# First block's last mixer products, norm and feed-forward input, done by halves of the tokens

## The reference

```python
y = jnp.concatenate([y_a, y_b, y_c], axis=-1) @ w_out[l]
x = x + gt1 * y
h = rms_norm(x, norm_ffn[l]) * (1.0 + sc2) + sh2
x = x + gt2 * conv_glu_ffn(h, ffn_w_up[l], ffn_conv_w[l], ffn_conv_b[l], ffn_w_down[l])
```

## Time and profile before

| | us |
|---|---|
| median of 3 runs (lowest, highest) | 2663.39 (2656.81, 2664.59) |
| the profiled execution, its own time | 2664.73 |
| its span | 2662.9 |
| PE busy | 2486.4 (93%) |
| DVE busy | 1452.2 (55%) |
| ACT, POOL busy | 876.1, 871.6 (33% each) |

### The profile page before, as it was taken

The page is one execution under the profiler, slowest core; times in us unless marked ns, Lnnn a source line. Parts: engine busy times, 40 slices in busy tenths (PEclk is TensorE's granted clock), DMA queues, the critical chain, the costliest instruction groups (busy, mean ns, idle before and its releaser), DMA issues.

```text
span 2662.9 us, 36956 instructions
## 1 busy us (share of the span) xinstructions
PE 2486.4 (93%) x15164; PEld 1455.5 (55%) x15164; DVE 1452.2 (55%) x1697; ACT 876.1 (33%) x1082; POOL 871.6 (33%) x494
## 2 busy tenths in 40 slices
PE   5899999999889999999998889999888999999996
PEld 2555558886445555555554556675344555555552
DVE  5764666773486630566325687355486640466413
ACT  3255422221144520445213222321155531354303
POOL 0212110000236531555215767201226532455320
PEclk7999999999989999999998889989999999999998
DMA  7611020000301133111312612300111122211311
GB/s 322 236 41 44 17 107 3 3 3 16 118 9 64 48 105 125 64 48 59 118 69 104 103 48 70 136 1 24 56 72 48 64 87 104 87 64 48 118 33 63
DMA packets 53497, 196.29 MB, mean 74 GB/s; under 512 B 5585, under 2 KB 15313, under 8 KB 50385
## 3 DMA queue, kind: packets, MB, share of 16 engines
q1 hardware_dynamic: 45552, 176.38, 19.5%
q10 hardware_dynamic: 7776, 17.56, 1.9%
HBM read 164.55 MB, written 29.36 MB: 73 GB/s over the span
## 4 chain that ended last, share of the span: by engine, by line
PE 80%; DVE 10%; issue 2%; POOL 2%; DMA 2%; ACT 2%; SPq 0%; ACTq 0%; DVEq 0%; POOLq 0%
PE pt L1138 15%; PE pt L1144 15%; PE pt L1141 15%; PE pt L1680 11%; PE pt L573 7%; PE pt L411 3%; PE pt L714 2%; PE pt L2391 2%; PE pt L2397 2%; PE pt L2394 2%; DVE work L536 1%; PE pt L344 1%; DMA work<-in_w_mod 1%; PE pt L332 1%; PE pt L397 1%
## 5 line engine op out<-in xcount | busy, mean ns | idle before, releaser
L1088 POOL TENSOR_TENSOR slots<-work,weights_rounded 128x512 bf16<-128x512 f32 (+2 forms) x234 | 420.7, 1798 | 598.5 <-ACT weights_rounded L1247 309.0
L1141 PE MATMUL pt<-work,weights_rounded 128*128 128x512 bf16 x1248 | 334.8, 386 | 0.0
L1138 PE MATMUL pt<-rounded,weights_rounded 128*128 128x512 f32 x624 | 210.1, 453 | 15.8 <-POOL slots L1088 10.2
L1138 PE MATMUL pt<-rhs_rounded,weights_rounded 128*128 128x512 f32 x624 | 210.2, 453 | 12.0 <-POOL slots L1088 7.8
L573 PE MATMUL pt<-work 64*64 64x64 f32 (+5 forms) x4512 | 208.0, 240 | 6.5 <-DVE work L536 5.5
L1138 PE MATMUL pt<-hidden_rounded,weights_rounded 128*128 128x512 f32 x704 | 207.2, 427 | 0.4
L573 PEld LDWEIGHTS pt<-work 64*64 64x64 f32 (+3 forms) x4512 | 188.7, 138 | 26.0 <-DVE work L536 7.7
L1141 PEld LDWEIGHTS pt<-work,weights_rounded 128*128 128x128 bf16 x1248 | 100.1, 99 | 169.0 <-issue 98.1
L1144 PE MATMUL pt<-hidden_rounded,slots 128*128 128x512 bf16 x704 | 179.9, 387 | 0.0
L1141 PE MATMUL pt<-slots,weights_rounded 128*128 128x512 bf16 x704 | 174.4, 381 | 0.0
L1144 PE MATMUL pt<-rounded,slots 128*128 128x512 bf16 x624 | 171.2, 390 | 0.0
(11 more groups left out here) (368 smaller groups left out, 4112.2 us busy)
## 6 DMA issues: line engine op xcount, KB each, us to landing
work<-in_w_up SPq DMA_DIRECT2D x64, 512.0 KB, 4.0
work<-in_w_down SPq DMA_DIRECT2D x32, 704.0 KB, 4.0
work<-in_w_mod SPq DMA_DIRECT2D x10, 2048.0 KB, 8.7
slots<-in_w_in SPq DMA_DIRECT2D x31, 512.0 KB, 3.6
slots<-in_w_up SPq DMA_DIRECT2D x24, 512.0 KB, 4.8
x_scratch<-work ACTq DMA_DIRECT2D x16, 512.0 KB, 2.6
work<-x_scratch SPq DMA_DIRECT2D x16, 512.0 KB, 8.0
slots<-in_w_v SPq DMA_DIRECT2D x10, 512.0 KB, 4.3
```

The source lines that it names most:

```text
L1088: did(pool, pool.tensor_tensor(dst, raw, high.bitcast(F32), ALU.subtract), name)
L1138: pe.matmul(out, whi[:, k * P:k * P + P], rhs_hi(k), start=first and k == ks[0], stop=False, skip_group_check=True)
L1141: pe.matmul(out, top_half(whi)[:, k * P:k * P + P], rhs_lo(k), start=False, stop=False, skip_group_check=True)
```

## The change

The eight products f are now formed for the first 512 tokens first (`f_part(0)` to `f_part(7)`) and then for the last 512 (`f_part(8)` to `f_part(15)`), one PSUM bank each. The sums and the spreading of 1/rms exist once for each half: `sums(0)` stands behind part 9, `rows(0)` behind part 10, `sums(1)` and `rows(1)` inside `ffn_pe`, as `between`. DVE and ACT handle 512 tokens in each operation, and DVE's list mixes the second half's additions with the first half's norm. In `ffn_pe`, plain group 0 is formed for the first half with whole tiles (24 matmuls for the gate, 24 for the value), and only its second half goes slice by slice.

POOL no longer waits for f4: it splits the two weight tiles of group 0 as soon as they are loaded, with their rests in slot 32. The tile after these, (1, 0), now waits until six slices of the second half are split. So that nothing else lives in those slots, `XP` moves from slots 42, 43, 44, 45, 46 to 44, 45, 46, 3, 4; slots 3 and 4 are free only when the mixer's recurrent core is done, so their DMA is issued after that. Apart from this the places of some tiles in the second block are moved, and some semaphores are merged.

```diff
-        XP = (42, 43, 44, 45, 46, 30, 31, 47)
+        XP = (44, 45, 46, 3, 4, 30, 31, 47)
...
+                    sp.wait_ge(E("chunk_done"), 3 * NC)
+                    sp.dma_start(W[:, XP[3]:XP[3] + 2, :], a["xT"][:, 3:5, :]).then_inc(E("x_in1"), 16)
...
-            for m in range(8):
-                linear(pe, f"f{m}", lambda k, m=m: woc[:, m, k * P:(k + 1) * P], YC,
-                       (lambda: pe.wait_ge(E("woc_in"), 128)) if m == 0 else None, ("y_c", 0) if m == 0 else None)
-            pe.wait_ge(E("square_sums"), 7)
-            token_sums(pe, "ss2", w(SQ2[0]), const("ones")[:, 0:1], 1)
-            token_rows(pe, "rb2", ("rstd_sqrt", 2), one_row)
-            ffn_pe(pe, 0)
+
+            def f_part(i):
+                h, m = divmod(i, 8)
+                if i < 8 and i % 2 == 0:
+                    claim(pe, f"f{i // 2}")
+                elif 8 <= i < 12:
+                    half_wait(pe, "dve", ("f", i - 4))
+                elif i >= 12:
+                    pe.wait_ge(E("pt_emptied_dve"), ordinal[f"f{i - 12}"])
+                if i == 0:
+                    pe.wait_ge(E("woc_in"), 128)
+                for k in range(3):
+                    if i == 0:
+                        pe.wait_ge(E("y_c"), k + 1)
+                    ins = pe.matmul(f_bank(i), woc[:, m, k * P:(k + 1) * P], w(YC[k])[:, half_of(h)], start=(k == 0),
+                                    stop=(k == 2))
+                ins.then_inc(E("pt_filled" if h else "half_pe"), 1)
+
+            def sums(h):
+                if h:
+                    pe.wait_ge(E("square_sums"), 7)
+                else:
+                    half_wait(pe, "dve", ("acc", 7))
+                for st in range(4):
+                    at = 512 * h + st * P
+                    ins = pe.matmul(f_sums(h)[:, st:st + 1], w(SQ2[0])[:, at:at + P], const("ones")[:, 0:1], start=True,
+                                    stop=True, skip_group_check=True)
+                ins.then_inc(E("pt_filled" if h else "half_pe"), 1)
+
+            def rows(h):
+                if h:
+                    pe.wait_ge(E("rstd_sqrt"), 2)
+                else:
+                    half_wait(pe, "act", "sqrt")
+                for st in range(4):
+                    ins = pe.matmul(f_rows(h)[:, st * P:(st + 1) * P], one_row(4 * h + st), const("ident"), start=True,
+                                    stop=True, skip_group_check=True)
+                ins.then_inc(E("pt_filled" if h else "half_pe"), 1)
+
+            for i in range(16):
+                f_part(i)
+                if i == 9:
+                    sums(0)
+                if i == 10:
+                    rows(0)
+            ffn_pe(pe, 0, (lambda: sums(1), lambda: rows(1)))
...
             for m in range(8):
-                filled(dve, f"f{m}")
-                V_(dve.scalar_tensor_tensor(w(X + m), pt(f"f{m}")[:, :], small(MOD + 16 + m), w(XP[m]), ALU.mult, ALU.add),
-                   "pt_emptied_dve")
-                add_square(dve, SQ2, 8, m - 1)
-            add_square(dve, SQ2, 8, 7)
-            rstd_dve(dve, "ss2", 1.0 / D, EPS)
-            filled(dve, "rb2")
+                f_added(0, m)
+                if m > 1:
+                    f_square(0, m - 1)
+            f_square(0, 7)
+            for m in range(8):
+                f_added(1, m)
+                if m > 1:
+                    f_square(1, m - 1)
+                if m == 1:
+                    f_recip(0)
+                if 4 <= m < 7:
+                    f_low(0, 2 * m - 8)
+                    f_low(0, 2 * m - 7)
+                for k in {3: (0, 1), 4: (2, 3), 5: (4, 5), 6: (6,)}.get(m, ()):
+                    f_scaled(0, k)
+            f_square(1, 7)
+            f_scaled(0, 7)
+            f_low(0, 6)
+            f_low(0, 7)
+            f_recip(1)
...
             for k in range(9):
                 if k < 8:
-                    V_(dve.scalar_tensor_tensor(w(SQ2[k]), w(X + k), small(G2 + k), pt("rb2")[:, :], ALU.mult, ALU.mult),
-                       "h_scaled" if k < 7 else "pt_emptied_dve")
+                    f_scaled(1, k)
...
+                if (j, g) == (1, 0) and t == 0:
+                    pool.wait_ge(E("rhs_split"), 8 + 6)
...
+            if between:
+                for g in range(2):
+                    pe.wait_ge(E("ffn_w_split"), plain_job(t, 0, g) + 1)
+                    claim_first(g)
+                    plain(0, (g,), range(8), (0,), lambda k: half_wait(pe, "dve", ("lo", k)))
+                    between[g]()
+                for k in range(8):
+                    pe.wait_ge(E("rhs_split"), 8 + 8 * t + k + 1)
+                    plain(0, (0, 1), (k,), (1,))
...
-            pool.wait_ge(E("pt_emptied_dve"), ordinal["f4"])
```

More of the change, by code:

```diff
@@ new lines, in f_square @@
+            def f_square(h, k):
+                seq = half_of(h)
+                if h:
+                    dve.wait_ge(E("squares"), 8 + k + 1)
+                    V_(dve.tensor_tensor(w(SQ2[0])[:, seq], w(SQ2[0])[:, seq], w(SQ2[k])[:, seq], ALU.add), "square_sums")
+                else:
+                    half_wait(dve, "act", ("sq", k))
+                    half_did(dve, dve.tensor_tensor(w(SQ2[0])[:, seq], w(SQ2[0])[:, seq], w(SQ2[k])[:, seq], ALU.add),
+                             "dve", ("acc", k))
@@ new lines, in f_low @@
+            def f_low(h, k):
+                seq = half_of(h)
+                if h:
+                    dve.wait_ge(E("rhs_hi"), 9 + k + 1)
+                elif k < 7:
+                    half_wait(dve, "act", ("hi", k))
+                else:
+                    dve.wait_ge(E("rhs_hi"), 8 + 1)
+                ins = dve.scalar_tensor_tensor(lo(HLO, k)[:, seq], w(SQ2[k])[:, seq], small(MOD + 24 + k),
+                                               hi(H + k)[:, seq].bitcast(F32), ALU.add, ALU.subtract)
+                if h:
+                    V_(ins, "rhs_split")
+                else:
+                    half_did(dve, ins, "dve", ("lo", k))
@@ L848, in build @@
         XSUM = (23, 38)
+        SQ3 = (26, 27, 28, 29, 30, 31, 48, 33)
         XB = (X, H)
@@ L920, in tile_raw @@
         def tile_raw(half, j, g):
-            return w(TILES[(2 * j + g) % 4])
+            slot = TILES[(2 * j + g) % 4]
+            return w(slot) if slot > 47 else M27[:, slot - 27, :]
         def down_raw(m):
@@ L1146, in passes, with plain @@
                 return ins
-            def plain(j, gs, ks):
+            def plain(j, gs, ks, hs=(0, 1), wait=None):
                 for g in gs:
-                    for h in range(2):
+                    for h in hs:
                         at = plain_at(j, g)
-                        ins = passes(up_pt(t, 0, j, g)[:, half_of(h)], flat_hi(at, D), flat_lo(at, D), ks,
+                        ins = passes(up_pt(t, 0, j, g)[:, half_of(h)], flat_hi(at, D), plain_lo(j, g), ks,
                                      lambda k: x_hi(t, k)[:, half_of(h)], lambda k: lo(HLO, k)[:, half_of(h)],
-                                     ks[0] == 0, ks[-1] == 7)
-                    if ks[-1] == 7:
+                                     ks[0] == 0, ks[-1] == 7, wait)
+                    if ks[-1] == 7 and 1 in hs:
                         ins.then_inc(E("ffn_w_used"), 1)
@@ L1202, in down @@
                 ins.then_inc(E("ffn_w_used"), 1)
[L1204 to L1209, removed]
+            if between:
[7 more added lines that the diff above has]
+                    plain(0, (0, 1), (k,), (1,))
+            else:
+                for g in range(2):
+                    pe.wait_ge(E("ffn_w_split"), plain_job(t, 0, g) + 1)
+                    claim_first(g)
+                for k in range(8):
+                    pe.wait_ge(E("rhs_split"), 8 + 8 * t + k + 1)
+                    plain(0, (0, 1), (k,))
             for g in range(2):
@@ L1925, in mixer2_pe @@
             out_part("b", lambda k: HR0[:, 4 + k, :], lambda k: lo(YRLO, k), "y_ret_split")
-            for t, sq, base in ((1, range(26, 34), 24), (2, range(0, 8), 32)):
+            for t, sq, base in ((1, SQ3, 24), (2, range(0, 8), 32)):
                 if t == 2:
@@ L2060, in mixer2_act @@
                 split_hi(n)
-            for t, sq in ((1, range(26, 34)), (2, range(0, 8))):
+            for t, sq in ((1, SQ3), (2, range(0, 8))):
                 for k in range(8):
```

130 lines of the change are left out of this document (104 added, 26 removed).

## The result

The changed kernel takes 2673.88 us (median of five, 2668.32 to 2678.06) against 2662.64 before (median of five): a ratio of 1.0043, interval 1.0032 to 1.0053. It is slower by 0.43%, some 11 us, by more than the 0.3% that can be told from no change.

What follows compares the result with a forecast made beforehand. The bound was the chain from the norm's last rest on DVE through ACT and POOL to PE. Terms 4.6 + 4.0 + 4.3 = 12.9 us gave 2677.6, stated as 2676.5 since the median is 1.3 lower; range 2662 to 2686.

Steps and rivals of the forecast that it cites:

- What bounds the stage: Norm's last rest on DVE, DVE's list, ACT, POOL, then PE: a 45.4 us chain in which PE has 7.8 us spare.
- Part 15 and PE's short steps: PE's products f: sums and rows between parts 9 and 11 add 2.2 us; part 15 done at 718.1.
- DVE's backlog: DVE behind part 11: 20.7 us of work, first half's last rest at 728.6, some 10 us after PE's last part.
- PE's passes and the low clock: PE behind that rest: gate 6.7 us with 5.8 at low clock, sums 1.3, value 5.5, rows 0.9, until 743.0.
- Halving and order together: Second half's norm on DVE: 12.5 us of operations, last rest at 755.5 instead of 750.90, 4.6 us later.
- Port, tile (1, 0): POOL's split of this tile makes DVE's last rests wait 1.6 and 2.35 us, together 4.0 us.
- Port, tile (1, 1): POOL's split of this tile blocks DVE's sums T1 and T3 for 4.75 us, against 0.4 before: 4.3 us more.
- a port shared by bandwidth: Alternative for POOL and DVE at SBUF: the 8.3 us of blocking would be some 4.
- Loads and second block at nothing: Later load of slots 3 and 4 is worth nothing, first read not before 624; second block only changes places, 0 us.
- PE's wait: PE's idle time before the fourth Strassen product: at 804 to 812, 14 to 20 us long.
- DVE keeps up: Rival, faster (0.12): first half's norm completes with part 15, PE makes no pause; about 2654 if POOL doesn't block either.
- no measurable change: Rival (0.24): the chain grows by less than 8 us, as DVE steps may be long and the port cost half.

Runs made afterwards that it cites:

- e4_split_alone: Kernel before, whole products, with only the change's moved XP, its loads, slot-32 rests and POOL's early split; tile (1, 0) after f2 is added: 2662.84 us, ratio 1.0000.
- e5_first_split_early: The change, with POOL's tile (1, 0) split once f2 is added instead of behind the sixth rest of the second half: 2675.29 us, ratio 1.0048.
- the first set: The kernels e1_last_split_later, e3_sums_first, e4_split_alone and b1_reordered, timed on one chip together with the kernel before, 2662.48 us there.
- e1_last_split_later: The change, with one more wait: POOL splits tile (1, 1) only after DVE's eight sums T1 and T3: 2669.36 us, ratio 1.0026.
- e3_sums_first: The change, with sums(1) and rows(1) of the second half ahead of group 0's first-half passes: 2659.48 us, ratio 0.9993.
- b1_reordered: The change, with sums(1) and rows(1) behind part 15, both POOL tiles' waits moved, group 0 in four whole-tile passes, DVE's and ACT's lists reordered: 2652.90 us, ratio 0.9958.
- b2_change_dve_order: b1_reordered, with DVE's and ACT's order as in the change: 2658.77 us, ratio 0.9989.
- e6_split_alone_later: e4_split_alone, with tile (1, 1) split only after the sums T1 and T3: 2663.64 us, ratio 1.0007.
- b3_both_blocks: b1_reordered, with tile (1, 1) split after the sums T1 and T3 in the second block too: 2655.75 us, ratio 0.9976.

## Why the prediction was right, step by step

The sign, the range and the mechanism were right. The sum was 12.9 us and the stage lost 10.65: each of its three terms was too large, by 1.0, 0.6 and 0.6 us, so no error was hidden by another. The forecast was 2.6 us above the median.

- **What bounds the stage.** Confirmed. PE's going on follows the last rest on DVE by 45.0 to 45.4 us in the seven kernels of the table where POOL meets neither T1 nor T3, and by 47.2 to 49.2 in the three where it does (the change, e4_split_alone, e5_first_split_early). The difference from before gives the median to 1 us for the change and the first set.
- **Part 15 and PE's short steps.** Predicted T0 + 43.5, measured 43.15: the sums took 0.95 and the rows 1.05 us, 2.0 in place of 2.2. The 0.16 us that I called the full-clock price of an L332 was wrong: the 48 at 624.29 ran at a granted clock of 0.68. In the changed kernel they ran at 1.00 and took 5.42 us, 0.11 each.
- **DVE's backlog.** The first half's last rest was predicted at T0 + 54.0 and came at 722.23, T0 + 54.3. PE's pauses were predicted at 8 us and came to 7.5 (3.05, 0.24 and 4.23).
- **PE's passes and the low clock.** From that rest to the sums the gate pass took 727.63 - 722.23 = 5.4 us, predicted 6.7. PE had begun on it at 721.39, and the granted clock was 0.51 from 721.4 to 725.4 and 1.00 from there to 729: 4.0 us of low clock, where I took 5.8. The sums took 0.8 us for 1.3, the value pass 5.5 as predicted. In all, the first scaling came at T0 + 67.19 for 68.4. The last rest, expected at 755 to 761 by the clock of the kernel before, came at 674.56 + 83.30 = 757.9.
- **Halving and order together.** The first scaling comes 67.19 - 55.28 = 11.91 us later than before (729.84 - 674.56 = 55.28), and the half list of DVE behind it is shorter. Without the port's 3.38 us (next point) the last rest would be 83.30 - 3.38 - 76.34 = 3.58 us later; predicted 4.6. The step was mis-sized by 1.0, mostly the 1.2 us by which the first scaling came early.
- **Port, tile (1, 0).** 5.02 us for two rests that take 1.64 in the same place in e5_first_split_early: +3.38, predicted 4.0. The first rest waited for the first operation's end, 747.89 - 746.19 = 1.7 us, where I had 1.6. That leaves 1.7 for the second, where I had all of its 2.35; it had begun at 747.97, before the second rest was due.
- **Port, tile (1, 1).** T1 grew by 4.13 us; the whole way from last rest to PE's going on grew by 49.10 - 45.41 = 3.69, predicted 4.3. e1_last_split_later takes 3.6 us back. The two together were 7.1, where I had 8.3; some 4, as a port shared by bandwidth would have given, is ruled out. The Trainium skill (SBUF — State Buffer, Who interferes with whom) states that a DVE instruction with two SBUF inputs contends with a GpSimd (POOL) instruction that reads SBUF, and that the shared ports are an exclusive lock. The trace agrees: T1 ends at 758.44, only 0.55 us, less than one sum, behind POOL's second operation (757.89).
- **Loads and second block at nothing.** Slots 3 and 4 are loaded from 606.67 and nobody waits for them: the addition of o3 at 621.20 waits for PE, 7.32 us. Confirmed.
- **PE's wait.** Predicted as one of 14 to 20 us ahead of the fourth Strassen product. It came as two, 7.87 us ahead of the first at 782.31 and 7.54 here, 15.4 in all. The size was right, the place was not: that POOL, behind ACT, would be late for the first product as well was not foreseen.
- **What was missed.** That a shift of DVE's list also shifts whom POOL meets stood in my rows and not in my argument; e4_split_alone showed it, with 5.34 us for T3.

Of the rivals, "DVE keeps up" fell (DVE was 11.2 us behind part 15), and "no measurable change" fell because both the port (7.1 us of 8.3) and the order (3.6 of 4.6) cost nearly their full price.

Beyond the prediction: the idea of halves was never the loss. e3_sums_first turns the sign of the stage by moving eight short matmuls (four sums and four rows, recorded as sixteen instructions), and b1_reordered shows what the halving can give. I had not asked which order would have won.

## What to carry to other kernels

Work that is put ahead of a short step of the deciding chain, on an engine that carries out its list in order, holds that step back when it is itself late: here by 9.9 us, for two passes of which 5.4 and 5.5 us stood ahead of it. Put the short steps first and fill behind them. Place POOL's operations on SBUF where DVE waits, or has an operand in PSUM, and look at whom they meet after every shift, since a gain of 1 us can put them onto the next sum (e4_split_alone). And take the marks of two traces from a point just ahead of the change, not from the start of the span.

## What the runs showed of the hardware

**The clock before the change.** Instructions that no kernel here changed ran at different granted clocks in the profiled executions. The 48 small matmuls at 624.29 took 7.74 us; in the changed kernel's profile the same ones took 5.42 us:

```profile
620.94 5.42 PE L361 MATMUL pt<-cst,work 128*128 128x2 f32 x48
```

In the other eight profiles they took 5.42 to 5.45 us three times (b2_change_dve_order, e5_first_split_early, b1_reordered), 6.69 once (e4_split_alone), 7.68 to 7.80 three times (e1_last_split_later, e3_sums_first, e6_split_alone_later) and 8.21 in b3_both_blocks. The mean granted clock of 612 to 634 us was 0.84 before, 0.92 in the change and 0.77 in e1_last_split_later. The start of the first product f lay between 667.91 and 676.35 in the ten profiles, a spread of 8.4 us, nearly as large as the effect of the change and about the spread of the runs. The halved kernels start it earlier (667.91 to 671.90) than the three with whole products (673.76 to 674.56), except b3_both_blocks, at 676.35. Each kernel has one profile only, so whether the kernel or the execution decides it is not shown.

**POOL and DVE block each other in turns.** A DVE operation with two inputs in SBUF waits for the end of POOL's, and that held for `scalar_tensor_tensor` (the rests, 5.02 us for two instead of 1.64; T3, 5.34 for four instead of 3.12) as for `tensor_tensor` (T1, 7.00 instead of 2.87). POOL pays too, less: its 128x1024 operation takes 2.35 us alone, 2.69 to 2.76 beside T1, where DVE's operations have 512 columns, and 3.34 behind a sum of 1024 that had just begun.
